# Start of a one-core transformer kernel: what each queue loads first, who issues it, and a second channel order for the router

## The chip, the core and the metric

One Trainium2 core runs the whole program in one launch. Its engines are TensorE (PE in the profile, with its weight loads shown apart as PEld), VectorE (DVE), ScalarE (ACT), GpSimd (POOL) and SyncE (SP), which here only issues transfers; 16 DMA engines move the data. Each engine runs its own instruction stream in order and waits on semaphores. The metric is the device time of one execution in microseconds, and the figure compared is the median of several executions.

## The reference

x is 256 tokens of 1024 channels in float32. What the start of the program has to do:

```python
x = x + pool_mixer(rms_norm(x, pool_norm), pool_w, pool_b, pool_scale)
x = x + hier_moe(rms_norm(x, ffn_norm[0]), router_group_w[0], ...)   # layer 0
k, k_rope, v = shared_kv(x, ...); x = x + mla_attention(...)
x = x + hier_moe(rms_norm(x, ffn_norm[1]), router_group_w[1], ...)   # layer 1
# then a second block: a mixer (S5 and mLSTM), cross attention to mem_2, a gated FFN
```

`pool_mixer` takes, for each quarter of the channels, a trailing mean (2, 4, 8 or 16 tokens) minus the token, multiplies by a 256x256 matrix, adds `pool_b` and scales by `pool_scale`. `hier_moe` chooses one of 4 groups and 2 of its 8 experts for each token from `h @ rg_w` and `h @ re_w`; each of the 32 experts computes `(silu(h @ w_gate) * (h @ w_up)) @ w_down`, 6 MiB of weights an expert. All 32 experts are computed in both layers.

## The kernel before

**Data.** Tokens lie on 128 partitions in two tiles (t = 0, 1): `X` is the residual, `XN` the normalised copy, `hT` and `pl` hold transposed activations with channels on partitions in 8 chunks k. `arena` is one large tile in which each stage has views of its own: `band` (the matrices of the trailing means, from `in_inverse_counts`), `pool_w`, `pool_b`, `pool_scale`, `memt` (the memory, from `in_mem`), `vec_rows` (small vectors, loaded as rows of 128 numbers and turned by PE into columns of `VT`), `rw` and `rb` (router weights and bias).

**Weights.** Everything large goes through `ring`, six places of 2 MiB each (a slab). SP issues the slabs in the order of their use, and before each it waits until PE has finished the slab that held the place (`slabs_done`). Slab `XK0` (a part of `x_wkv`) is first, then five expert slabs fill the ring. At each MoE some extra slabs find room outside of the ring: one in the arena (`load_ahead`, after x is ready), one over `X` once `X` is parked in DRAM (`park_x`, then `load_over_x`), one over `XN` after sorting (`load_over_sorting`, L638). From the fourth turn on the loads run in a loop.

**The first stage.** SP issues `X`, 7 small vectors, `pool_w`, then 13 more vector loads, three S5 vectors, `memt`, four router loads. Then it waits for all small vectors (`vec2_loaded`) and the pool data (`pool_loaded`), and only then issues `XK0` and the slabs. ACT issues `const`, `band`, `pool_b`, `pool_scale`, `ffn_gain` from its own queue.

The work is: ACT sums squares of X (`norm("pool")`, L1539), DVE scales it into `XN` (L1922), PE multiplies by the bands (L831, L832), DVE and ACT evict (L1931, L1550), PE multiplies by `pool_w` (L841). POOL first waits for all three pool loads, multiplies `pool_b` by `pool_scale` (L2582), waits for the S5 vectors and copies one (L2584), and adds the bias to X (L2589, two instructions). DVE waits for both and for the norm of the memory, and adds the mixer's output in four pairs (L1961, L1962). The last pair makes x ready (`x_ready`).

**Router.** PE turns X (L751, `turn(X)`, 16 transposes), turns the memory in layer 0, and multiplies by `rw` (L868). `hT[p, k]` holds channel 128k + p, so `rw` is loaded as `"(k p) g -> p k g"`: for every partition 8 pieces of 16 or 128 bytes. DVE chooses, PE counts (L885 to L889), DVE builds the selection matrices, and PE sorts the tokens (L899) and starts on the experts (L956 gate and up, L972 transposes, L1000 down, L985 combination). L899 reads `XN_rows`, where chunk c holds channels 8p + c: its weight operand has a stride of 8 numbers. L972 reads `hid_rows` with a stride of 2. In the gaps PE computes the memory's keys (L796). `keep_busy` (L818) issues matmuls whose results nobody reads.

## Time and profile before

| | us |
|---|---|
| median of 3 runs | 1698.14 (1697.07 to 1698.57) |
| the profiled execution | 1701.85 |
| its span, from first to last instruction | 1700.0 |
| PE busy | 1612.9 (95%) |
| DVE, ACT, POOL busy | 456.6, 234.5, 97.3 |
| the chain that ended last | PE 63%, DMA 30%, DVE 4%, ACT 1% |
| moved | 512.48 MB, 301 GB/s over the span |

The profile cuts the span into 40 slices of 42.5 us: through the two MoE layers the DMA engines are busy all the time at 420 to 428 GB/s; in the attention part between them and behind the second they are not. The chain of work that ended last is followed back from the last instruction: at each step to what released it. Busy time of an engine off that chain costs nothing. The profiled execution is 3.71 us longer than the median of the runs.

### The profile page before, as it was taken

The numbers are of one execution on the slowest core, as the hardware profiler recorded it, in microseconds if no ns is written. First come the engines' busy times: TensorE is split into PE (matmuls) and PEld (weight loads), VectorE is DVE, ScalarE is ACT, GpSimd is POOL, SyncE is SP. The second block draws the span as 40 slices with busy tenths as digits, with TensorE's granted clock in tenths as the row PEclk, the third lists the DMA queues.
The fourth block names the chain that finished last, engine by engine and source line by source line (L and its number), as shares of the span: only waits on it lengthen the run. The fifth ranks groups of instructions, "written<-read, shape, count | busy, mean of one in ns | idle before, by whom it ended". The sixth has DMA issues, their size and how long they took to land.

```text
span 1700.0 us, 22104 instructions
## 1 busy us (share of the span) xinstructions
PE 1612.9 (95%) x9079; PEld 1008.2 (59%) x9079; DVE 456.6 (27%) x983; ACT 234.5 (14%) x519; POOL 97.3 (6%) x165
## 2 busy tenths in 40 slices
PE   8999998888989999999998988999999998999998
PEld 7755544444446766755544444448578777688843
DVE  4311111111113323212111111115976302344411
ACT  4110100000002121111000000013122113100000
POOL 2300000000000000029200000000000000000000
PEclk9999999999999999999999999998999999999999
DMA  9999999999998643899999999998324451444400
GB/s 330 419 412 423 426 428 426 425 425 426 427 421 299 197 173 125 347 406 419 426 426 427 427 428 426 426 386 308 124 100 149 179 167 50 161 149 148 149 25 25
DMA packets 107944, 512.48 MB, mean 301 GB/s; under 512 B 17034, under 2 KB 46315, under 8 KB 74091
## 3 DMA queue, kind: packets, MB, share of 16 engines
q1 hardware_dynamic: 105595, 506.24, 74.4%
q10 hardware_dynamic: 2288, 5.40, 0.9%
q8 instruction: 41, 0.67, 0.2%
q14 instruction: 20, 0.16, 0.0%
HBM read 506.38 MB, written 5.24 MB: 301 GB/s over the span
## 4 chain that ended last, share of the span: by engine, by line
PE 63%; DMA 30%; DVE 4%; ACT 1%; SPq 1%; issue 1%; DVEq 0%; ACTq 0%
DMA ring<-in_w_up 29%; PE PS L956 15%; PE PS L1480 9%; PE PS L1000 5%; PE PS L1224 4%; PE PS L1492 4%; PE PS L985 3%; PE PS L1235 2%; PE PS L899 2%; PE PS L1430 2%; PE PS L811 2%; PE PS L1203 2%; PE PS L1407 2%; PE PS L796 1%; DMA ring<-in_x_wkv 1%; PE PS L1416 1%
## 5 line engine op out<-in xcount | busy, mean ns | idle before, releaser
L956 PE MATMUL PS<-ring,arena 128*64 128x256 f32 x3968 | 449.2, 381 | 54.8 <-DMA ring<-in_w_up 42.7
L956 PEld LDWEIGHTS PS<-ring,arena 128*64 128x64 f32 x3968 | 287.7, 137 | 236.7 <-DMA ring<-in_w_up 60.0
L1000 PE MATMUL PS<-ring,arena 128*64 128x512 f32 x992 | 226.5, 598 | 1.2 <-ACT arena L1659 1.2
L2116 DVE TENSOR_TENSOR arena<-PS,arena 128x256 f32<-128x256 f32 x64 | 27.2, 424 | 719.7 <-ACT arena L1651 719.7
L1000 PEld LDWEIGHTS PS<-ring,arena 128*64 128x64 f32 x992 | 66.2, 136 | 152.9 <-issue 152.1
L1480 PE MATMUL PS<-hT,ring 128*128 128x256 f32 x640 | 138.3, 379 | 0.0
L1480 PEld LDWEIGHTS PS<-hT,ring 128*128 128x128 f32 x640 | 121.6, 190 | 16.5
L985 PE MATMUL PS<-arena,hT 64*128 64x512 f32 x512 | 127.2, 615 | 1.2 <-ACT arena L1668 1.2
L1659 ACT ACTIVATE arena<-PS 128x256 f32<-128x256 f32 x64 | 24.6, 384 | 507.7 <-PE PS L972 507.7
L1224 PE MATMUL PS<-hT,ring 128*128 128x256 f32 x384 | 86.7, 387 | 0.0
L1224 PEld LDWEIGHTS PS<-hT,ring 128*128 128x128 f32 x384 | 74.2, 195 | 11.7 <-issue 1.5
L1668 ACT ACTIVATE arena<-PS 128x512 f32<-128x512 f32 x64 | 38.2, 597 | 306.2 <-PE PS L1000 306.2
L1492 PE MATMUL PS<-ring,arena 128*128 128x512 f32 x176 | 75.7, 592 | 0.0
L985 PEld LDWEIGHTS PS<-arena,hT 64*128 64x128 f32 x512 | 44.1, 186 | 39.9 <-issue 30.2
L1492 PEld LDWEIGHTS PS<-ring,arena 128*128 128x128 f32 x176 | 33.4, 190 | 41.7 <-issue 41.4
L2128 DVE SCALAR_TENSOR_TENSOR hT<-hT,arena 128x512 f32<-128x512 f32 x64 | 50.5, 789 | 0.4 <-PE PS L985 0.2
L2307 DVE SCALAR_TENSOR_TENSOR arena<-PS,VT,arena 128x255 f32<-128x255 f32 (+2 forms) x104 | 43.5, 476 | 1.1
L2302 DVE TENSOR_SCALAR arena<-PS,VT 128x256 f32<-128x256 f32 x48 | 23.0, 537 | 77.5 <-PE PS L1480 77.4
L2110 DVE COPY arena<-arena 128x512 f32 (+1 forms) x64 | 28.7, 449 | 29.2 <-issue 22.2
L972 PEld LDWEIGHTS PS<-const,arena 128*128 128x128 f32 x128 | 20.4, 206 | 24.8 <-issue 24.7
L899 PE MATMUL PS<-arena,XN 128*128 128x256 f32 x128 | 32.3, 409 | 1.0 <-DVE arena L2041 1.0
L899 PEld LDWEIGHTS PS<-arena,XN 128*128 128x128 f32 x128 | 31.2, 335 | 3.2 <-issue 3.0
(424 smaller groups left out, 1445.1 us busy)
## 6 DMA issues: line engine op xcount, KB each, us to landing
ring<-in_w_gate SPq DMA_DIRECT2D x62, 2048.0 KB, 25.5
ring<-in_w_up SPq DMA_DIRECT2D x62, 2048.0 KB, 25.6
ring<-in_w_down SPq DMA_DIRECT2D x62, 2048.0 KB, 24.6
ring<-in_f_w_up SPq DMA_DIRECT2D x22, 1024.0 KB, 7.4
ring<-in_w_in SPq DMA_DIRECT2D x9, 2048.0 KB, 19.0
ring<-in_f_w_down SPq DMA_DIRECT2D x5, 2048.0 KB, 7.8
arena<-in_w_gate SPq DMA_DIRECT2D x2, 2048.0 KB, 22.7
ring<-in_x_wkv SPq DMA_DIRECT2D x2, 2048.0 KB, 8.4
```

Of the source, the lines that this page charges most:

```text
L811: mm = pe.matmul(PS[:, 1, :], hT[:, k, t * P:(t + 1) * P], w[:, k, :], start=(k == 0), stop=(k == KD - 1))
L899: mm = pe.matmul(PS[:, 4 * half + c // 2, c % 2 * T:(c % 2 + 1) * T], XN_rows[:, t, c, :], sel[:, t, half * T:(half + 1) * T], start=(t == ...
L956: mm = pe.matmul(PS[half * WINDOW:(half + 1) * WINDOW, bank, m * half_f:(m + 1) * half_f], xw[bank][:, k, :], mat(k, F_EXP)[:, half * half ...
L985: mm = pe.matmul(PS[:, 4 + 2 * t + half, :], buf[rows, t * P:(t + 1) * P], y2[rows, :], start=first, stop=last, skip_group_check=True)
L1000: mm = pe.matmul(PS[half * WINDOW:(half + 1) * WINDOW, 3, :], hidT[:, w, k * WINDOW:(k + 1) * WINDOW], mat(k, D)[:, half * 512:(half + 1) ...
L1203: mm = pe.matmul(PS[:, 2 + 2 * half + t, :], oT[:, h, t * P:(t + 1) * P], w[:, h, :], start=(h == 0), stop=(h == HEADS - 1))
L1224: mm = pe.matmul(PS[:, bank + b, f % 2 * T:(f % 2 + 1) * T], w[:, k, f * P:(f + 1) * P], x[:, k, :], start=(k == 0), stop=(k == kx - 1))
L1480: mm = pe.matmul(PS[:, 2 * (j % 2) + h, f * T:(f + 1) * T], w[:, k, h, f * P:(f + 1) * P], x[:, k, :], start=(k == 0), stop=(k == KD - 1))
L1492: mm = pe.matmul(PS[:, 4 + 2 * t + half, :], gF[:, c, t * P:(t + 1) * P], w[:, c - 4 * j, half * 512:(half + 1) * 512], start=(c == 0), st ...
L1668: act.activation(y2, PS[:, 3, :], ACT.Copy).then_inc(g["y_sbuf"], 1)
L2128: dve.scalar_tensor_tensor(gates2, slots[:, 0, :], slot_of[:, w, bass.ds(linear(e, 1, 0), 1)], slots[:, 1, :], ALU.is_equal, ALU.mult).the ...
L2307: ins = dve.scalar_tensor_tensor(v, ps(f)[:, 0:T - back], taps[f][back], v, ALU.mult, ALU.add)
```

## The change

It does seven things.

- `X` is loaded in two halves, by SP and ACT, each the first transfer of its queue; both halves count on `x_loaded` (waits on it rise by one transfer).
- SP issues, behind its half, 6 small vectors and `pool_w`, and at once `XK0` and five expert slabs. Its wait for `vec2_loaded` and `pool_loaded` is gone.
- The other 13 vector loads and the three S5 vectors are issued by POOL, ahead of all its work, all on `vec2_loaded`.
- `memt` is issued by ACT behind `pool_scale`; the four router loads of layer 0 by ACT behind `norm("pool")`. Layer 1's stay with SP.
- The router rows are loaded as `"(p k) g -> p k g"`, contiguous in each partition. So `hT` of both routers must hold channel 8p + k: `turn(X, rows=X_rows)` reads X with a stride of 8 numbers, and the gain comes from `ffn_gain` instead of `VT`. `ffn_norm` leaves the small vectors.
- `eps` no longer comes with `const` but from a DVE memset into a tile of its own; ACT no longer waits for `const` before the first norm, and DVE does `norm("pool")` before it copies the first vectors.
- PE's first `keep_busy` (8 matmuls on `const`) becomes 20 matmuls on a tile that DVE sets to one.

The core of the diff (the rest moves semaphore counts by what is listed above):

```diff
-VECTORS = (("pool_norm", 8), ("ffn_norm", 16), ("kv_in_norm", 8), ("attn_norm", 8), ("kv_norm", 2),
+VECTORS = (("pool_norm", 8), ("kv_in_norm", 8), ("attn_norm", 8), ("kv_norm", 2),
...
-FIRST_VECTORS = 7
+FIRST_VECTORS = 6
+SECOND_LOADS = len(VEC_PARTS) - FIRST_VECTORS + 3
...
+        eps_at = sbuf("eps_at", [P, 1])
...
+        warm = hTf[:, 0:P]
+        X_rows = X[:, :, :].rearrange("p t (q k) -> p t k q", k=KD)
...
+        def vectors(eng, parts, loaded):
+            for name, first, at, m in parts:
+                src = a[name]
+                dims = " ".join(f"a{i}" for i in range(len(src.shape)))
+                src = src.rearrange(f"{dims} -> ({dims})").rearrange("(r p) -> r p", p=P)
+                eng.dma_start(vec_rows[at % P:at % P + m, at // P, :], src[first:first + m, :]).then_inc(s[loaded], 16)
+        def router_loads(eng, layer):
+            eng.dma_start(rw[:, :, 0:GROUPS], a["router_group_w"][layer].rearrange("(p k) g -> p k g", p=P)).then_inc(s["row_loaded"], 16)
+            eng.dma_start(rw[:, :, GROUPS:], a["router_expert_w"][layer].rearrange("(p k) g -> p k g", p=P)).then_inc(s["row_loaded"], 16)
+            eng.dma_start(rb[:, 0:GROUPS], a["router_group_b"][layer].partition_broadcast(P)).then_inc(s["row_loaded"], 16)
+            eng.dma_start(rb[:, GROUPS:], a["router_expert_b"][layer].partition_broadcast(P)).then_inc(s["row_loaded"], 16)
-            sp.dma_start(X[:, :, :], a["x"].rearrange("b (t p) d -> p (b t) d", p=P)).then_inc(s["x_loaded"], 16)
-            def vectors(parts, loaded):
-                for name, first, at, m in parts:
-                    src = a[name]
-                    dims = " ".join(f"a{i}" for i in range(len(src.shape)))
-                    src = src.rearrange(f"{dims} -> ({dims})").rearrange("(r p) -> r p", p=P)
-                    sp.dma_start(vec_rows[at % P:at % P + m, at // P, :], src[first:first + m, :]).then_inc(s[loaded], 16)
-            vectors(VEC_PARTS[:FIRST_VECTORS], "vec_loaded")
+            sp.dma_start(X[:, 0, :], a["x"].rearrange("b (t p) d -> p (b t) d", p=P)[:, 0, :]).then_inc(s["x_loaded"], 16)
+            vectors(sp, VEC_PARTS[:FIRST_VECTORS], "vec_loaded")
-            vectors(VEC_PARTS[FIRST_VECTORS:], "vec2_loaded")
-            for at, name in ((0, "s5_lam_re_2"), (S5J, "s5_lam_im_2")):
-                sp.dma_start(s5_rows[at:at + S5J, :], a[name][0].rearrange("(j g) p -> j (g p)", g=2)).then_inc(s["s5_loaded"], 16)
-            sp.dma_start(ldt2[32:32 + S5J, :], a["s5_log_dt_2"][0].rearrange("(j g) -> j g", g=2)).then_inc(s["s5_loaded"], 16)
-            def router_loads(layer):
-                sp.dma_start(rw[:, :, 0:GROUPS], a["router_group_w"][layer].rearrange("(k p) g -> p k g", p=P)).then_inc(s["row_loaded"], 16)
-                sp.dma_start(rw[:, :, GROUPS:], a["router_expert_w"][layer].rearrange("(k p) g -> p k g", p=P)).then_inc(s["row_loaded"], 16)
-                sp.dma_start(rb[:, 0:GROUPS], a["router_group_b"][layer].partition_broadcast(P)).then_inc(s["row_loaded"], 16)
-                sp.dma_start(rb[:, GROUPS:], a["router_expert_b"][layer].partition_broadcast(P)).then_inc(s["row_loaded"], 16)
-            sp.dma_start(memt, a["mem_2"].rearrange("b (t p) d -> p (b t) d", p=P)).then_inc(s["mem_loaded"], 16)
-            router_loads(0)
-            sp.wait_ge(s["vec2_loaded"], 16 * (len(VEC_PARTS) - FIRST_VECTORS))
-            sp.wait_ge(s["pool_loaded"], 16 * 3)
-                router_loads(1)
+                router_loads(sp, 1)
...
-            def turn(v, bank=4):
+            def turn(v, bank=4, rows=None):
-                            mm = pe.transpose(PS[:, bank + j, at:at + P], v[:, t, c * P:(c + 1) * P], ident)
+                            part = v[:, t, c * P:(c + 1) * P] if rows is None else rows[:, t, c, :]
+                            mm = pe.transpose(PS[:, bank + j, at:at + P], part, ident)
...
+            pe.wait_ge(s["dve_step"], 2)
+            for _ in range(20):
+                pe.matmul(PS[:, 7, 0:P], warm, warm, start=True, stop=True)
-            keep_busy(7, 8)
...
-                turn(X)
+                turn(X, rows=X_rows)
...
+            act.dma_start(X[:, 1, :], a["x"].rearrange("b (t p) d -> p (b t) d", p=P)[:, 1, :]).then_inc(s["x_loaded"], 16)
+            act.dma_start(memt, a["mem_2"].rearrange("b (t p) d -> p (b t) d", p=P)).then_inc(s["mem_loaded"], 16)
...
-            act.wait_ge(s["x_loaded"], 16)
+            act.wait_ge(s["dve_step"], 2)
+            act.wait_ge(s["x_loaded"], 32)
+            norm("pool")
+            router_loads(act, 0)
-            norm("pool")
...
-                hT_upper(name, ["ffn_norm"], KD * layer)
+                act.wait_ge(s["gain_loaded"], 16)
+                hT_upper(name, ["ffn_norm"], col=router_gain(layer))
...
-            dve.wait_ge(s["x_loaded"], 16)
+            step(dve.memset(eps, EPS))
+            step(dve.memset(warm, 1.0))
+            dve.wait_ge(s["x_loaded"], 32)
+            norm("pool")
-            norm("pool")
...
-                hT_lower(name, ["ffn_norm"], KD * layer)
+                dve.wait_ge(s["gain_loaded"], 16)
+                hT_lower(name, ["ffn_norm"], col=router_gain(layer))
...
+            vectors(pool, VEC_PARTS[FIRST_VECTORS:], "vec2_loaded")
+            for at, name in ((0, "s5_lam_re_2"), (S5J, "s5_lam_im_2")):
+                pool.dma_start(s5_rows[at:at + S5J, :], a[name][0].rearrange("(j g) p -> j (g p)", g=2)).then_inc(s["vec2_loaded"], 16)
+            pool.dma_start(ldt2[32:32 + S5J, :], a["s5_log_dt_2"][0].rearrange("(j g) -> j g", g=2)).then_inc(s["vec2_loaded"], 16)
-            pool.wait_ge(s["s5_loaded"], 16 * 3)
+            pool.wait_ge(s["vec2_loaded"], 16 * SECOND_LOADS)
```

The order on ACT's stream, from its start, before:

```order
L1525 DMA const<-in_const 128x1193
L1526 DMA arena<-in_inverse_counts 128x1536
L1527 DMA arena<-in_pool_b 128x1024
L1528 DMA arena<-in_pool_scale 128x1024
L1530 DMA ffn_gain<-in_ffn_norm 128x2x8
L1535 ACT_TABLE_LOAD [waits const_loaded]
L1535 ACTIVATE stat<-const 1x1 [waits x_loaded]
```

and after:

```order
L1519 DMA X<-in_x 128x1024
L1520 DMA const<-in_const 128x1192
L1521 DMA arena<-in_inverse_counts 128x1536
L1522 DMA arena<-in_pool_b 128x1024
L1523 DMA arena<-in_pool_scale 128x1024
L1524 DMA arena<-in_mem 128x2x1024
L1526 DMA ffn_gain<-in_ffn_norm 128x2x8
L1531 ACT_TABLE_LOAD [waits x_loaded]
L1531 ACTIVATE stat<-eps_at 1x1 [waits dve_step]
L1535 ACTIVATE XN,stat<-X 128x1024
L1537 ACTIVATE stat<-stat,eps_at 128x1 [waits norm_ssq]
L1535 ACTIVATE XN,stat<-X 128x1024
```

X's half stands ahead of `const`, the memory has come in behind `pool_scale`, and the table load now waits for `x_loaded` instead of `const_loaded`.

The order on SP's stream around `pool_w` and the first slabs, before (its tail ahead of the first slabs):

```order
L551 DMA arena<-in_s_lam_im 16x128
L552 DMA arena<-in_s_log_dt 16x2
L560 DMA arena<-in_mem 128x2x1024
L555 DMA arena<-in_router_group_w 128x8x4
L556 DMA arena<-in_router_expert_w 128x8x32
L557 DMA arena<-in_router_group_b 128x4
L558 DMA arena<-in_router_expert_b 128x32
L579 DMA ring<-in_x_wkv 128x8x384 [waits pool_loaded,vec2_loaded]
L597 DMA ring<-in_w_gate 128x4096
L597 DMA ring<-in_w_up 128x4096
```

and after, from `pool_w` on:

```order
L541 DMA arena<-in_mem_norm_g 8x128
L556 DMA arena<-in_pool_w 128x8x256
L571 DMA ring<-in_x_wkv 128x8x384
L589 DMA ring<-in_w_gate 128x4096
L589 DMA ring<-in_w_up 128x4096
L589 DMA ring<-in_w_gate 128x4096
L589 DMA ring<-in_w_up 128x4096
L589 DMA ring<-in_w_down 128x2x2048
L606 DMA x_park<-X 128x2048 [waits x_ready]
L589 DMA arena<-in_w_gate 128x4096 [waits x_ready]
```

Between `pool_w` and `ring<-in_x_wkv` no transfer and no wait is left.

The order on POOL's stream at its first arithmetic, before:

```order
L2571 UNCONDITIONAL_BRANCH [waits barrier_Pool_Activation_PE_DVE_SP_gather]
L2582 ISA
L2582 TENSOR_TENSOR arena<-arena 128x1024 [waits pool_loaded]
L2584 COPY arena<-arena 16x128 [waits s5_loaded,pool_step]
L2589 TENSOR_TENSOR X<-X,arena 128x1024 [waits norm_xn,s5_small]
```

and after (ten vector loads stand ahead of this piece):

```order
L541 DMA arena<-in_f_conv_w 127x128
L541 DMA arena<-in_f_conv_w 5x128
L541 DMA arena<-in_f_conv_b 44x128
L2588 DMA arena<-in_s_lam_re 16x128
L2588 DMA arena<-in_s_lam_im 16x128
L2589 DMA arena<-in_s_log_dt 16x2
L2591 ISA
L2591 TENSOR_TENSOR arena<-arena 128x1024 [waits pool_loaded]
L2593 COPY arena<-arena 16x128 [waits vec2_loaded,pool_step]
L2598 TENSOR_TENSOR X<-X,arena 128x1024 [waits norm_xn,s5_small]
```

The multiplication now stands behind 16 transfers that POOL issues itself, and its copy waits for all of them instead of three.

## Rows read from the trace of the kernel before

**Rows 1.** Chain that ended last, in order of time: start, us, what; first MoE.

```profile
33.08 3.50 PE PS L868 x32
...
46.63 8.01 PE PS L899 x32
...
203.01 6.93 PE PS L956 x64
...
209.96 22.67 DMA ring<-in_w_up
```

**Rows 2.** Windows: busy us of five engines with counts, granted clock, DMA share, GB/s.

```profile
core 0: us, PE busy (x) PEld busy (x) DVE busy (x) ACT busy (x) POOL busy (x), PEclk, DMA share, GB/s
4.00:8.00 4.00, 1.51 (x7) 1.51 (x8) 0.00 (x0) 1.28 (x1) 0.00 (x0) 1.00 1.02 417
...
20.00:24.00 4.00, 4.00 (x20) 3.54 (x19) 0.33 (x3) 3.17 (x9) 3.83 (x2) 1.00 0.47 72
...
100.00:104.00 4.00, 4.00 (x40) 2.61 (x38) 0.00 (x0) 0.60 (x1) 0.00 (x0) 1.00 0.90 305
...
728.00:732.00 4.00, 4.00 (x36) 2.44 (x34) 0.00 (x0) 0.60 (x1) 0.00 (x0) 1.00 0.74 238
```

**Rows 3.** SyncE issues in order of time: start, us, queue, line, transfer.

```profile
88.30 0.43 SPq L638 DMA_DIRECT2D arena<-in_w_down  x1
100.30 0.33 SPq L597 DMA_DIRECT2D ring<-in_w_gate  x1
```

**Rows 4.** Timeline, first stage: start, us, engine, line, what, [idle before <-releaser].

```profile
1.23 0.49 ACTq L1526 DMA_DIRECT2D arena<-in_inverse_counts  x1
...
2.23 0.80 ACTq L1528 DMA_DIRECT2D arena<-in_pool_scale  x1
...
6.49 3.49 PEld L818 LDWEIGHTS PS<-const 128*128 128x128 f32 x16 [6.49 <-DMA const<-in_const]
...
6.52 1.28 ACT L1535 ACT_TABLE_LOAD   x1 [6.52 <-DMA const<-in_const]
...
8.88 0.20 ACT L1535 ACTIVATE stat<-const 1x1 f32<-1x1 f32 x1 [1.08 <-DMA X<-in_x]
...
15.96 2.35 POOL L2582 TENSOR_TENSOR arena<-arena 128x1024 f32<-128x1024 f32 x1 [15.52 <-DMA arena<-in_pool_w]
...
18.81 0.28 POOL L2584 COPY arena<-arena 16x128 f32<-16x128 f32 x1 [0.50 <-DMA arena<-in_s_log_dt]
...
19.17 4.66 POOL L2589 TENSOR_TENSOR X<-X,arena 128x1024 f32<-128x1024 f32 x2
...
28.62 0.69 DVE L1962 TENSOR_TENSOR X<-X,arena 128x512 f32<-128x512 f32 x1
```

**Rows 5.** DMA issues by transfer: KB each, us from issue to landing.

```profile
arena<-in_inverse_counts ACTq DMA_DIRECT2D x1, 768.0 KB, 8.3
...
arena<-in_pool_scale ACTq DMA_DIRECT2D x1, 512.0 KB, 11.0
```

**Rows 6.** The page's part on DMA queues: kind, packets, MB, share.

```profile
q10 hardware_dynamic: 2288, 5.40, 0.9%
```

**Rows 7.** Weight loads of three lines: ns min/median/max, first and last start.

```profile
L751 PEld LDWEIGHTS PS<-const,X x48: 138/140/144, 29.4 to 662.9; 128*128 128x128 f32 x48
...
L899 PEld LDWEIGHTS PS<-arena,XN x128: 312/336/338, 46.6 to 710.8; 128*128 128x128 f32 x128
...
L972 PEld LDWEIGHTS PS<-const,arena x128: 194/198/223, 82.5 to 1136.0; 128*128 128x128 f32 x128
```

**Rows 8.** Chain that ended last, second MoE, router: start, us, what.

```profile
661.50 1.75 PE PS L751 x16
663.24 1.73 PE PS L796 x8
664.97 3.51 PE PS L868 x32
```

**Rows 9.** Windows of one us, same columns as rows 2, first router stage.

```profile
38.00:39.00 1.00, 1.00 (x4) 0.82 (x3) 0.90 (x6) 0.21 (x1) 0.00 (x0) 0.50 0.96 410
```

More of the change, by code:

```diff
@@ L121, in constants @@
     put("causal_mask", np.where(col <= row, 0.0, -BIG))
-    put("eps", np.full((P, 1), EPS))
     window_row = np.arange(P)[:, None] % WINDOW + WINDOW * np.arange(WINDOWS)[None, :]
@@ L368, in bc @@
             return v.to_broadcast([P, *shape])
-        ident, ones, eps = cc("ident"), cc("ones"), cc("eps")
+        ident, ones, eps = cc("ident"), cc("ones"), eps_at[:, 0:1]
         ssq, rms, rinv = stat[:, 0:2], stat[:, 2:4], stat[:, 4:6]
@@ L618, in load_over_x @@
                     name = ("ffn0", "ffn1")[layer]
-                    sp.wait_ge(s["x_loaded"], 16 * (2 + 2 * layer))
+                    sp.wait_ge(s["x_loaded"], 16 * (3 + 2 * layer))
                     sp.wait_ge(s["norm_xn"], TT * (SCALED.index(name) + 1))
@@ L1240, in mix @@
             def mix():
[L1241 removed]
+                pe.wait_ge(s["s5_loaded"], 16 * 9)
                 for ri in range(2):
@@ L1541, in norm, with router_gain @@
                     act.activation(rms[:, t:t + 1], ssq[:, t:t + 1], ACT.Sqrt, bias=eps, scale=1.0 / D).then_inc(s["norm_rms"], 1)
+            def router_gain(layer):
+                return lambda name, c: ffn_gain[:, layer, c:c + 1]
             def hT_upper(name, gains, at=0, dsts=(hT,), bank=4, col=vec):
@@ L1922, in norm, with router_gain @@
                         dve.tensor_scalar(XN[:, t, :], src[:, t, :], rinv[:, t:t + 1], None, ALU.mult).then_inc(s["norm_xn"], 1)
+            def router_gain(layer):
+                return lambda name, c: ffn_gain[:, layer, c:c + 1]
             def hT_lower(name, gains, at=0, dsts=(hT,), bank=4, col=vec):
@@ L2159, in experts @@
                         step_dve(dve.tensor_tensor(gains, PS[:, 0, 0:KD], VT[:, at:at + KD], ALU.mult))
-                    dve.wait_ge(s["x_loaded"], 16 * (3 + 2 * layer))
+                    dve.wait_ge(s["x_loaded"], 16 * (4 + 2 * layer))
                     dve.wait_ge(s["proj_mm"], 2 * TT + layer + 1)
```

10 lines of the change are left out of this document (3 added, 7 removed).

## Prediction, made before the changed kernel ran

> **What bounds the kernel now.** I read the chain of waits first. In the first MoE it runs over PE alone from the router (33.08) over the sort (46.63) to 203.01; from 209.96 on it waits for slabs, one of 22.67 us at first [rows 1]. So PE works on a stock of slabs early and uses it up later; behind 210 the DMA engines set the time. It looks as if 17 us of earlier slab loads must be worth 17 us. But the ring has six places, and the windows tell when it was full: from 100 to 104 us the DMA share is 0.90 and the rate 305 GB/s, where the stretch from 4 to 8 us has 1.02 and 417 [rows 2]. SP had issued at 88.30 and next at 100.30, when PE freed a place [rows 3]: DMA had nothing to do then for about a us. All later slabs queue behind that issue, so the end of the first MoE moves with the moment at which PE frees that place (100.30), and that moves with the moment at which x is ready. A slab that is there earlier only makes DMA idle longer. The second MoE has the same hole at 728 to 732 (0.74, 238 GB/s) [rows 2]. So two things count: when x is ready (29.31, the end of the last addition at 28.62 + 0.69 [rows 4]), and PE's way from there to the experts, in both layers.
>
> What makes x ready: `pool_w` lands at 15.96 and starts POOL (2.35 us, to 18.31); POOL waits 0.50 us for an S5 vector, adds the bias to X (19.17 + 4.66 = 23.83), and DVE's additions follow until 29.31 [rows 4].
>
> **How the queues share the engines.** ACT's queue moved 2288 packets [rows 6]. Its 15 transfers have 2048 contiguous pieces, and 15 x 16 completions are 240: a packet is one piece. A transfer of one piece for each of 128 partitions gives 8 to each of the 16 engines. Now the landings, per engine: ACT's 8th piece (`const`) at 6.49; X, 16 pieces on SP's queue, at 8.86 [rows 4]; ACT's 16th piece (`band`) at 1.23 + 8.3 = 9.5; the 32nd (`pool_scale`) at 2.23 + 11.0 = 13.2 [rows 4, 5]. X and ACT's 16th piece land within 0.7 us, though band's pieces are 6 KB and X's 4 KB. The queues take turns piece by piece, not byte by byte. That matters, since `pool_w` comes in 8 pieces of 1 KB a partition, 64 an engine.
>
> **Part by part.**
>
> *X in halves.* Both halves go first: 1.05 MB before anything else. X lands some 2.5 us sooner (2.36 us lay between `const` and X [rows 4]). The table load, which hid ahead of X, now waits for X and costs its 1.28 us [rows 4]. DVE no longer waits for the first vectors. The normalised X is ready 1.5 to 2 us earlier, and PE's band matmuls with it. PE then waits for `pool_w`; this gain ends there and is worth 0.
>
> *pool_w.* Behind its half of X, ACT's queue holds 8 + 8 + 8 + 8 + 16 + 16 = 64 pieces an engine (`const`, `band`, `pool_b`, `pool_scale`, memory, `ffn_gain`); SP's holds about 3 + 64. One for one they end together. Before, the memory's 1.05 MB came behind `pool_w`; now they go ahead: 1.05 MB at 417 GB/s [rows 2] is 2.5 us. POOL's own queue adds 316 short pieces, 20 an engine; at the 0.057 us of a `pool_w` piece alone ((15.96 - 13.2) / 48) this would be 1.1 us, at their bytes 0.4; I take 0.8. `pool_w` lands at 15.96 + 2.5 + 0.8 = 19.3. Below, it can't start POOL before `pool_scale`, 13.2 plus the 1.2 us of ACT's half of X: 14.4. Above: SP's queue loses more turns, 21.
>
> *POOL's 16 issues.* No row shows one. SP's take 0.33 and 0.43 us [rows 3], which for 16 gives 5 to 7 us; longer ones can't be excluded. They are hidden while they end before 19.3, up to 1.2 us each. So 0, and the wait of 0.50 us for the S5 vector goes: -0.5. The Trainium skill (DMA: Bandwidth & Descriptors, Specifications) gives the GpSimd path about 1 us to the first byte; if each issue held POOL so long they would end at 17, and the sum would be the same. No run so far shows it.
>
> *x ready:* +3.3 - 0.5 = **+2.8 us**, at 32.1. Bounds: -2.0 (14.4) and +4.5 (21).
>
> *Turning X with a stride of 8.* The operand read with a stride is PE's weight load. Contiguous, a transpose's load shows 140 ns (L751) and the pace is 1.75 / 16 = 109 ns [rows 7, 8]. With a stride of 2 (L972) it shows 198, with a stride of 8 (L899, not a transpose) 336 [rows 7], and L899's pace is 8.01 / 32 = 250 ns [rows 1], where its 256 columns alone need 216 (1.73 us for 8 in L796 [rows 8]). So the load sets 250. I take it, since stride and operand are those of the new line: 16 x (250 - 109) = **+2.2 us**. Lower bound by L972: 16 x 58 ns = 0.9. Nothing hides it: PE goes on in order to L868, whose result DVE waits for. It is paid in both layers: in the second the chain runs L751, L796, L868 without a gap [rows 8]. The Trainium skill (SBUF — State Buffer, Door 1: The DMA port swizzle) speaks of 16-byte lines in which at least two accesses are needed for full speed: a stride of 2 float32 would be free, a stride of 8 not. The trace disagrees on the first (198 against 140) and agrees on the second; by the rule the lower bound would not exist, and the sum would stand.
>
> *Router rows.* 128 short pieces an engine become 16. They land before the large slabs if ACT issues them by 12 us: ACT's 64 + 32 pieces then end ahead of SP's 3 + 64 + 64. L868 began at 33.08 before [rows 1]. Worth 0, since the ring's hole takes the freed DMA time. Layer 1's stay off the chain in the attention part.
>
> *eps, warm-up, gains, removed SP waits:* 0; they lie before `pool_w`, or touch slabs that arrive early.
>
> **Sum:** 2.8 + 2.2 (layer 0) + 2.2 (layer 1) = +7.2 us. The profiled execution would be 1701.85 + 7.2 = 1709.1; it stood 3.7 above the median, so the median becomes 1698.1 + 7.2 = **1705.3**.
>
> **Rivals.**
>
> 1. *The head start counts* (the side that is not slower). From 20 to 24 us DMA had a share of 0.47 at 72 GB/s [rows 2]: 2.1 us idle, and the rest on small router pieces. Some 4 us of slab traffic could come earlier. If the stock never fills the ring, the first MoE ends 4 us sooner whatever PE does at first: 1698.1 - 4 + 2.2 = 1696.3, or 1694.1 with a free stride. It decides where DMA had no hole before 100.30; the hole is there. 0.12, of which 0.07 below 1694.7.
> 2. *The stride is free in a transpose*: only +2.8, 1700.9. For: the 336 ns are of a plain load, and no row has a transpose with a stride of 8. Against: L972 is a transpose and pays. 0.10.
> 3. *pool_w is not late*, since ACT's queue runs behind or yields: x ready at -2.0 to 0, the stride paid twice: 1700.5 to 1702.5, say 1701.5. Against: the landings fit turns by piece within 0.7 us. 0.13.
> 4. *The clock.* At 38 to 39 us it stood at 0.50 (1.2 GHz) [rows 9], behind a stretch from 29.3 to 36.6 in which PE had only transposes and L868's 36 columns [rows 1, 4]. That stretch is now 2.2 us longer, and PE's fillers ahead of it end about when they did while x comes 2.8 us later, so it begins behind an idle PE. If the half clock takes in L868 (3.50 us [rows 1]) as well: some +3, 1708.3. 0.10.
>
> My forecast has 0.55, with 1702 to 1709 of its own.
>
> **How the numbers follow.** About 0.2% (3.4 us) is what a measurement of this kernel can tell from no change. Slower by more: forecast and rival 4 (0.65) and a part of rival 3: 0.68. Faster: 0.07 from rival 1. Same: 0.25. The lower end takes in the lower bounds of both terms (-2.0 + 0.9 + 0.9: 1697.9) and rivals 2 and 3; the upper end +4.5 + 4.4 and some clock: 1710. Outside lie rival 1 and the tails, less than 0.2.
>
> **What would show it.** POOL's multiplication starts, released by `pool_w`, near 19.3 (rival 3: before 16.5). The last addition ends near 32.1. The 16 transposes of X take 4.0 us instead of 1.75 in both layers (rival 2: under 2.5). SP's first issue out of the ring's hole comes near 105 instead of 100.30, with a lower DMA share before it (rival 1: share 1.0 throughout). `const` lands near 8, the router rows near 22. What would make it wrong: a large first slab that ACT's pieces must take turns with, if `pool_w` were ahead of them all (router rows after 35 us, much slower), or POOL issues over 1.2 us each.

## The result, and the profile of the changed kernel

| | median | lowest to highest | runs | profiled execution: time, span |
|---|---|---|---|---|
| before | 1698.16 us | 1697.07 to 1698.57 | 4 | 1701.85, 1700.0 |
| after | 1729.01 us | 1728.09 to 1729.61 | 4 | 1729.21, 1727.2 |

The changed kernel is slower: the ratio is 1.0171, with a 95% interval from 1.0153 to 1.0190. The prediction was 1705.3 us in a range of 1697.9 to 1710.0. The direction was right and the size was not: 31 us instead of 7. Of the 31, the two causes that it gave make 3: `pool_w` came late, and the stride cost nothing.

The spans lie 27.2 us apart, the medians 30.8. The profiled execution of before was 3.7 us above its median, so the traces can explain only the 27.2.

The first view is again the chain of waits, now of the changed kernel (start, us, what), in its first MoE. L863 is the router's matmul (L868 before), L950 the experts'.

```profile
19.89 37.64 DMA arena<-in_router_expert_b
57.53 0.04 issue
57.57 7.04 PE PS L863 x32
...
86.85 7.06 PE PS L950 x64
...
237.87 22.57 DMA ring<-in_w_up
```

In [rows 1] the chain ran over PE from 33.08. Here it sits on one DMA for 37.64 us: the last of the four transfers of layer 0's router rows, 16 KB on ACT's queue. PE begins its router matmuls at 57.57, and they take 7.04 us where they took 3.50.

The timeline of the first stage, the same columns as [rows 4] (L546 and L547 are the last two router loads on ACT's queue, L589 the expert slabs on SP's, L591 POOL's product, L1967 DVE's last addition, L744 the transposes of X):

```profile
4.95 10.87 SPq L589 DMA_DIRECT2D ring<-in_w_gate  x1
...
5.96 1.28 ACT L1531 ACT_TABLE_LOAD   x1 [5.96 <-DMA X<-in_x]
...
11.76 8.10 ACTq L546 DMA_DIRECT2D arena<-in_router_group_b  x1
...
19.48 2.34 POOL L2591 TENSOR_TENSOR arena<-arena 128x1024 f32<-128x1024 f32 x1 [9.47 <-DMA arena<-in_pool_w]
19.89 1.07 ACTq L547 DMA_DIRECT2D arena<-in_router_expert_b  x1
...
31.66 0.69 DVE L1967 TENSOR_TENSOR X<-X,arena 128x512 f32<-128x512 f32 x1
32.41 2.06 PE L744 MATMUL PS<-const,X 128*128 128x128 f32 x16 [1.20 <-DVE X L1967]
...
57.57 7.04 PE L863 MATMUL PS<-arena,hT 128*128 128x36 f32 x32 [21.36 <-DMA arena<-in_router_expert_b]
```

`pool_w` starts POOL at 19.48 (15.96 in [rows 4]) and x is ready at 31.66 + 0.69 = 32.35. The 16 transposes of X take 2.06 us. Then PE idles for 21.36 us, until the rows are there. Two issues stall their queues: 10.87 us on SP, 8.10 us on ACT.

The DMA issues by transfer (KB, us from issue to landing) and the page's part on queues, which answer to [rows 5] and [rows 6]:

```profile
arena<-in_router_expert_w ACTq DMA_DIRECT2D x1, 128.0 KB, 40.5
...
arena<-in_router_expert_w SPq DMA_DIRECT2D x1, 128.0 KB, 8.2
```

```profile
q10 hardware_dynamic: 5072, 7.14, 1.2%
```

The same 128 KB take 40.5 us on ACT's queue in layer 0 and 8.2 us on SP's in layer 1, ahead of SP's later slabs. ACT's queue moved 5072 packets, 2784 more than in [rows 6]. That number tells what the rows were cut into: half of X (128), memory (256), two bias rows (128 + 128) and six more completions of 16 make 736; the other 2048 are the two row matrices, 1024 each, which is 8 pieces a partition and not one.

The windows, the same columns as [rows 2]:

```profile
core 0: us, PE busy (x) PEld busy (x) DVE busy (x) ACT busy (x) POOL busy (x), PEclk, DMA share, GB/s
36.00:40.00 4.00, 0.22 (x2) 0.00 (x0) 2.24 (x6) 2.67 (x5) 0.00 (x0) 1.00 1.01 422
...
44.00:48.00 4.00, 0.00 (x0) 0.00 (x0) 0.00 (x0) 0.00 (x0) 0.00 (x0) 0.50 1.02 406
56.00:60.00 4.00, 2.43 (x12) 2.43 (x12) 0.00 (x0) 0.00 (x0) 0.00 (x0) 0.50 0.03 9
60.00:64.00 4.00, 4.00 (x21) 4.00 (x20) 0.00 (x0) 0.00 (x0) 0.00 (x0) 0.50 0.02 4
...
80.00:84.00 4.00, 4.00 (x19) 3.79 (x19) 0.84 (x3) 2.25 (x5) 0.00 (x0) 1.00 0.00 0
124.00:128.00 4.00, 4.00 (x20) 1.20 (x18) 1.51 (x3) 0.00 (x0) 0.00 (x0) 1.00 0.77 324
```

While PE waits, DMA works at full share on slabs (422 and 406 GB/s). It stops when everything is in (0.03 from 56 to 60) and stands still at 80 to 84 (0.00). The ring's last slab, issued at 17.40, landed after 32.5 us, at 49.9; the last of the router rows landed at 57.5: the slabs came first and the few bytes that PE needed came last. The granted clock falls to 0.50, the lower of PE's two levels, 1.2 GHz, while PE idles, and is still there when the router's matmuls run. That is why they take 7.04 us.

SP's issues around the ring's hole answer to [rows 3]:

```profile
116.20 0.43 SPq L630 DMA_DIRECT2D arena<-in_w_down  x1
128.21 0.33 SPq L589 DMA_DIRECT2D ring<-in_w_gate  x1
```

100.30 has become 128.21, by 27.9 us. The second MoE's router (as [rows 8]) and the weight loads of the transposes (as [rows 7]):

```profile
688.93 1.76 PE PS L744 x16
690.70 1.73 PE PS L789 x8
692.42 3.50 PE PS L863 x32
```

```profile
L744 PEld LDWEIGHTS PS<-const,X x48: 139/188/207, 32.4 to 690.3; 128*128 128x128 f32 x48
```

The 16 transposes with a stride of 8 take 1.76 us in the chain, against 1.75 without it.

### The profile page after: what moved, and what is told of

It reads as the page before. It is cut to its first block, busy times and chain, and to the rows that moved or that the text cites. A ratio compares the mean times of both kernels' runs of the same rounds, so it can differ in the third digit from the quotient of the medians.

```text
span 1727.2 us, 22153 instructions
## 1 busy us (share of the span) xinstructions
PE 1621.5 (94%) x9103; PEld 1015.7 (59%) x9103; DVE 457.6 (26%) x985; ACT 234.2 (14%) x519; POOL 106.2 (6%) x181
## 3 DMA queue, kind: packets, MB, share of 16 engines
q10 hardware_dynamic: 5072, 7.14, 1.2%
## 4 chain that ended last, share of the span: by engine, by line
PE 60%; DMA 33%; DVE 4%; ACT 1%; SPq 1%; ACTq 1%; issue 1%; DVEq 0%
DMA ring<-in_w_up 29%; PE PS L950 14%; PE PS L1474 9%; PE PS L1218 4%; PE PS L1486 4%; PE PS L994 4%; PE PS L1229 2%; DMA arena<-in_router_expert_b 2%; PE PS L979 2%; PE PS L893 2%; PE PS L1424 2%; PE PS L1197 2%; PE PS L804 2%; PE PS L1401 2%; PE PS L789 1%; DMA ring<-in_x_wkv 1%
## 5 line engine op out<-in xcount | busy, mean ns | idle before, releaser
L950 PE MATMUL PS<-ring,arena 128*64 128x256 f32 x3968 | 449.2, 381 | 55.1 <-DMA ring<-in_w_up 42.9
L950 PEld LDWEIGHTS PS<-ring,arena 128*64 128x64 f32 x3968 | 287.6, 137 | 237.0 <-DMA ring<-in_w_up 60.2
L2121 DVE TENSOR_TENSOR arena<-PS,arena 128x256 f32<-128x256 f32 x64 | 27.2, 425 | 719.2 <-ACT arena L1652 719.2
L1474 PEld LDWEIGHTS PS<-hT,ring 128*128 128x128 f32 x640 | 121.6, 190 | 16.5
L1486 PEld LDWEIGHTS PS<-ring,arena 128*128 128x128 f32 x176 | 33.4, 190 | 41.7 <-issue 41.4
L789 PE MATMUL PS<-arena,ring 128*128 128x256 f32 x128 | 32.6, 410 | 1.1 <-DMA ring<-in_x_wkv 1.1
```

The costliest lines, as they stand in the source:

```text
L789: mm = pe.matmul(PS[:, bank, col + i * T:col + (i + 1) * T], w[:, k, f * P:(f + 1) * P], x[:, k, :], start=(k == 0), stop=(k == KD - 1), s ...
L950: mm = pe.matmul(PS[half * WINDOW:(half + 1) * WINDOW, bank, m * half_f:(m + 1) * half_f], xw[bank][:, k, :], mat(k, F_EXP)[:, half * half ...
L1474: mm = pe.matmul(PS[:, 2 * (j % 2) + h, f * T:(f + 1) * T], w[:, k, h, f * P:(f + 1) * P], x[:, k, :], start=(k == 0), stop=(k == KD - 1))
L1486: mm = pe.matmul(PS[:, 4 + 2 * t + half, :], gF[:, c, t * P:(t + 1) * P], w[:, c - 4 * j, half * 512:(half + 1) * 512], start=(c == 0), st ...
```

## The experiments

What they had to tell apart: is the wait made by ACT's short pieces taking turns with SP's large ones (piece for piece), and which of three things decides it: who is in which queue, how many pieces there are, or how large the other queue's pieces are? Then each smaller term of the sum was tried by itself. Line numbers in the variants differ by a few.

All in one table. "Router" is the start of the router's first matmul in layer 0, "hole" SP's issue out of the ring's hole, "sort 2" the start of the sort in the second MoE, all in us of the profiled run. The kernel before was timed again beside each group: 1698.74 us (e1, e2, e3, e8), 1698.95 (e4, e6, e7, e9) and 1699.37 (e5, e10, e11, e12).

| run | median | ratio to before, 95% | router | hole | sort 2 |
|---|---|---|---|---|---|
| before | | | 32.92 | 100.30 | 677.70 |
| after | 1729.01 | 1.0171 [1.0153, 1.0190] | 57.57 | 128.21 | 705.73 |
| e1, rows on SP's queue | 1707.36 | 1.0052 [1.0032, 1.0072] | 37.62 | 106.41 | 682.23 |
| e2, slabs wait for rows | 1705.76 | 1.0045 [1.0028, 1.0062] | 36.13 | 103.95 | 681.57 |
| e3, slabs in 4 KB pieces | 1707.37 | 1.0049 [1.0033, 1.0065] | 36.20 | 105.23 | 683.94 |
| e8, rows in whole runs | 1704.07 | 1.0038 [1.0022, 1.0053] | 35.79 | 103.08 | 678.84 |
| e4, before, SP doesn't wait | 1699.40 | 1.0001 [0.9993, 1.0010] | 33.95 | 100.53 | 677.97 |
| e5, before, stride of 8 | 1698.66 | 1.0000 [0.9989, 1.0011] | 33.82 | 100.39 | 676.96 |
| e12, before, POOL's queue | 1700.62 | 1.0011 [1.0002, 1.0021] | 34.39 | 103.28 | 680.60 |
| e6, e1 with memory behind | 1705.23 | 1.0036 [1.0024, 1.0048] | 33.58 | 102.52 | 680.28 |
| e7, e6 with waits split | 1702.75 | 1.0027 [1.0016, 1.0037] | 31.71 | 100.70 | 675.98 |
| e9, e7 with whole runs | 1702.91 | 1.0026 [1.0014, 1.0038] | 33.03 | 101.70 | 679.08 |
| e10, e7 with more fillers | 1699.76 | 1.0002 [0.9992, 1.0012] | 31.96 | 98.58 | 674.23 |
| e11, e9 with fillers, rows on ACT | 1700.79 | 1.0009 [0.9998, 1.0020] | 33.43 | 100.06 | 675.97 |

One thing first. From the hole to the sort of the second MoE it is 575.3 to 578.7 us in all fourteen rows (577.4 before, 577.5 after). Whatever moves the hole moves all that follows, to within these 3.4 us. Times of the trace are those of one execution, medians those of 4 to 35.

### e1: the router rows on SP's queue

```diff
             sp.dma_start(pool_w, ...).then_inc(s["pool_loaded"], 16)
+            router_loads(sp, 0)
...
-            router_loads(act, 0)
```

> The changed kernel with layer 0's four router loads issued by SP between pool_w and the first slab instead of by ACT. Theory (turns): the router rows are still cut into 8 short pieces a partition, because their place in SBUF is (8 rows of 36 numbers, 4 and 32 of them filled by different loads), so ACT's queue had 144 pieces an engine left which took turns one for one with SP's 16 KB pieces until SP's stock was used up. Ahead of the slabs on SP's own queue they land near 25 us, PE's router matmuls start right behind the transposes (about 36 us instead of 57.6) at full clock, and the time is 1729.0 - 21.4 - 3.4 = about 1703 (1701 to 1705). Rival (early slabs as such): whatever the router's queue, slabs issued at 4 us crowd the rest out; the time stays over 1715.

Measured 1707.36 us, above the 1701 to 1705 expected, hole at 106.41. The wait of 21 us is gone, so the rows' place in the queues makes it. The hole is 2.5 us later than e2's, and two rows of its timeline say where:

```profile
32.60 3.44 PE L745 MATMUL PS<-const,X 128*128 128x128 f32 x16 [2.88 <-DVE X L1967]
...
65.84 6.26 PE L951 MATMUL PS<-ring,arena 128*64 128x256 f32 x55 [1.73 <-issue]
```

The transposes of X came behind 2.88 us of idle PE and took 3.44 us, not 2.06 (granted clock 0.57 from 32 to 36 us). And PE stalled for 1.73 us after the ninth matmul of the first expert, on nothing that the profile names.

### e2: SP's slabs wait for the rows

```diff
+            sp.wait_ge(s["row_loaded"], 64)
```

> The changed kernel, but SP waits for layer 0's router rows before it issues the first slab; the rows stay on ACT's queue. Theory (turns): without large pieces on the other queue the router rows land at about 25 us, 1703 us in all (1701 to 1706), since slabs that start at 26 us are still there before PE needs them. Rival (ACT's issue stall of 8.1 us at the group bias, or ACT's queue being slow by itself): the rows still land after 40 us, the slabs come later still, and the time is over 1730.

Measured 1705.76 us, as expected. The rows are still 128 + 16 short pieces an engine on ACT's queue, and still behind everything there; only SP's large ones stay away until they are in. SP's first slab is issued at 23.11, so the rows had landed by then, not at 57.5. The pieces' number alone doesn't hurt. It takes the large ones beside them.

### e3: the first four expert slabs in pieces of 4 KB

```diff
+                        for c in range(4):
+                            cols = slice(c * 1024, (c + 1) * 1024)
+                            sp.dma_start(slab(n0 + j)[:, cols], (gate, up)[m][e][:, cols])...
```

> The changed kernel with the first four expert slabs issued as four transfers each, so that their pieces are 4 KB instead of 16 KB; same bytes, same queue. Theory (turns by piece): SP's stock has 64 + 128 + 16 + 8 + 8 pieces an engine instead of 128 in all, and ACT's 144 are through when about as many of SP's are: the last router load lands near 40 us instead of 57.5, the time falls by 15 to 20 us to 1709 to 1714. Rival (turns by byte, or an issue stall): no change, 1729.

Measured 1707.37 us, faster than the 1709 to 1714 expected. Nothing is moved and nothing waits; the slabs are the same bytes, in pieces of a quarter:

```profile
arena<-in_router_expert_w ACTq DMA_DIRECT2D x1, 128.0 KB, 22.4
...
36.20 4.27 PE L870 MATMUL PS<-arena,hT 128*128 128x36 f32 x32
```

The same 128 KB land after 22.4 us, not 40.5. The last of the four row transfers lands at 36.2 (19.67 + 16.5), where 40 was expected, and PE, whose transposes end at 36.20 too, doesn't wait any more. This is the sharpest of the tests: if the queues shared by bytes, cutting SP's pieces smaller would change nothing for ACT. They take turns by piece. SP's issues also came later here (its ring was issued by 33.4 us instead of 17.8), but that didn't clear the way: from 20 to 36 us the DMA share stays at 1.04 or more and the rate at 350 to 398 GB/s, so SP's pieces were there all the time.

### e8: the rows in whole runs, into a free place

```diff
+        rstage = arena[:, 19000:19000 + KD * (GROUPS + EXPERTS)]
...
+                eng.dma_start(stage_e, a["router_expert_w"][layer].rearrange("(p k) g -> p (k g)", p=P))...
...
+            step(pool.tensor_copy(rw[:, :, GROUPS:], stage_e.rearrange("p (k g) -> p k g", k=KD)))
```

> The changed kernel with layer 0's router rows loaded to a contiguous place (one piece of 128 bytes and one of 1 KB a partition) from where GpSimd copies them into their 8 rows; still on ACT's queue, still behind the first norm. Theory (turns, and the number of pieces): 32 pieces an engine instead of 144 on ACT's queue, through before SP's first 16 KB piece; the rows land at 22 to 24 us and the time is about 1702 (1701 to 1705). Rival (the number of pieces doesn't matter, only which queue): the rows land after 45 us and the time stays over 1720.

Measured 1704.07 us, as expected. Everything stays where the change has put it, on ACT's queue and beside SP's slabs, but the place that the rows are written to is contiguous too:

```profile
q10 hardware_dynamic: 3280, 7.14, 1.1%
...
arena<-in_router_expert_b ACTq DMA_DIRECT2D x1, 16.0 KB, 10.6
```

1792 packets fewer than the changed kernel's 5072 is 2 x (1024 - 128), to the packet: one piece a partition for each matrix. The last row transfer is issued at 11.46 and lands 10.6 us later, at 22.1. The prediction had said "the router rows near 22". Its arithmetic was right for 16 pieces an engine; the changed kernel has 128. ACT's issue stall of 8.10 us is gone as well (0.62 here). x is ready at 32.11, 2.8 us later than before, and the hole at 103.08, later by the same 2.8, although SP issues the first slab at 4.76 instead of 21.46.

### e4: the kernel before, with SP's two waits taken out

```diff
-            sp.wait_ge(s["vec2_loaded"], 16 * (len(VEC_PARTS) - FIRST_VECTORS))
-            sp.wait_ge(s["pool_loaded"], 16 * 3)
```

> The kernel before without SP's two waits ahead of the slabs; everything else as before, so SP issues the keys' weights and the first slabs as soon as it has issued the router rows. Theory (the ring's hole sets the end of the first MoE): a head start of the slabs is worth nothing, 1698 within 2 us, SP's issue out of the hole still at 100.3 within 0.5, DMA share between 24 and 100 us emptier at its end. Rival 1 of the prediction (the head start counts): about 4 us faster, 1694. On turns by piece: SP's slabs are all behind the router rows on the same queue, so the rows aren't late and the router still starts at 33.1.

Measured 1.0001, hole at 100.53. In its windows DMA still has a share of 0.46 from 20 to 24 us and of 0.80 from 100 to 104, the hole. But SP issues `XK0` at 21.06, where it did so at 21.03 before: its two waits had never held the slabs up. Its own issues had, the longest of them 3.96 us for `in_router_group_b` at 16.49. So e4 gives no head start and doesn't test what one is worth. The changed kernel and e8 do: they issue the first slab 16 us earlier and the ring's last 7 us earlier, and the hole moves by what PE's path moves, 27.9 and 2.8 us.

### e5: the kernel before, with the stride alone

```diff
-                turn(X)
+                turn(X, rows=X_rows)
...
-    a["router_expert_w"][layer].rearrange("(k p) g -> p k g", p=P)
+    a["router_expert_w"][layer].rearrange("(p k) g -> p k g", p=P)
```

> The kernel before with the stride alone: transposes of X read columns 8 apart, the router rows of both layers are laid in to match, and the gain comes from ffn_gain. The prediction's step said 16 loads of 250 ns in place of 109 in both layers, +4.4 us: 1703. What the changed kernel's trace shows (1.76 us for 16) says +0.0 to +0.2: 1699, the 16 transposes of X under 2.2 us in layer 0 and 1.8 in layer 1. A third outcome: the router rows read as contiguous runs of 8 rows change their landing; it stays off the path, as before.

Measured 1.0000 [0.9989, 1.0011]. Its chain in the second MoE:

```profile
660.15 1.78 PE PS L753 x16
```

The stride costs 0.03 us for 16, in place of the 2.2 predicted. The same run says what the new order of the rows does to the transfers. SP's queue in the page of the kernel before, and then in that of e5:

```profile
q1 hardware_dynamic: 105595, 506.24, 74.4%
```

```profile
q1 hardware_dynamic: 105595, 506.24, 74.3%
```

Not one packet fewer: read as `"(p k)"`, the rows are cut into as many pieces as before.

### e12: the kernel before, with the second vectors on POOL's queue

```diff
-            vectors(VEC_PARTS[FIRST_VECTORS:], "vec2_loaded")
+            for name, first, at, m in VEC_PARTS[FIRST_VECTORS:]:
+                ...
+                pool.dma_start(vec_rows[at % P:at % P + m, at // P, :], src[first:first + m, :])...
```

> The kernel before with one part of the change alone: the nine second vectors and the S5 ones (16 transfers) are issued on GpSimd's queue at its start instead of SP's behind pool_w. Theory of the prediction: the issues take about 0.5 us each and end near 10 us, ahead of pool_w at 16, so nothing on the path moves later; pool_w at 15.96 to 16.8 and the wait of 0.50 us for an S5 vector goes: 1698 to 1699, 0 to -0.5. Rival (something of GpSimd's own queue costs time that the profiled stretch doesn't show, since the variants e6, e7 and e9 take 3 to 5 us more by their medians than their first 100 us explain): 1700 to 1703, with a wider spread of times than before.

Measured 1.0011 [1.0002, 1.0021]: 0.3 to 3.6 us slower by the interval, more than the 0 to -0.5 expected, and with no wider spread (6.6 us from lowest to highest, 7.7 for the kernel before). The timeline:

```profile
9.12 0.48 POOL L2583 DMA_DIRECT2D arena<-in_s_log_dt  x1
17.42 2.35 POOL L2585 TENSOR_TENSOR arena<-arena 128x1024 f32<-128x1024 f32 x1 [7.82 <-DMA arena<-in_pool_w]
...
39.19 5.82 PE L792 MATMUL PS<-arena,ring 128*128 128x256 f32 x14
```

POOL's issues end at 9.6 and are hidden. But `pool_w` lands at 17.42, where it landed at 15.96, 16.64 (e4) and 16.13 (e5) with those transfers on SP's queue behind it. A third queue that takes turns costs `pool_w` 0.8 to 1.5 us, from one profile of each. The 14 matmuls of the memory's keys also drew the half clock (5.82 us; e4 and e5 have 3.29, the profile of before 4.98). Of these 2.5 us some 1.9 reach the hole, which is 2.9 us later than in e5; in e5 PE waits 0.66 us for DVE behind them. That draw differs from run to run.

### e6, e7, e10: three repairs, one upon the other

```diff
 e6, upon e1
-            act.dma_start(memt, ...)
+            sp.dma_start(memt, ...)            (behind pool_w, ahead of the router rows)
 e7, upon e6
-            pool.wait_ge(s["pool_loaded"], 16 * 3)      (POOL and DVE)
+            pool.wait_ge(s["pool_loaded"], 16 * 2)
+            pe.wait_ge(s["out_stored"], 16)             (PE alone waits for pool_w)
 e10, upon e7
-                    keep_busy(7, 13)
+                    keep_busy(7, 17)
```

> The changed kernel with the router rows of layer 0 on SP's queue (as in e1) and the memory there too, behind pool_w and ahead of the router rows. What it tests: the term for pool_w, 2.5 us of it from the memory's 1.05 MB ahead of pool_w. Theory: pool_w lands near 17.0 instead of 19.68, x is ready near 30.0 instead of 32.5, SP's issue out of the ring's hole comes near 104 instead of 106.41, and the time is about 2.5 us below e1's 1707.4: 1704 to 1706. Rival (the landing of pool_w is due to the issue order or POOL's own transfers, not the memory): pool_w stays at 19 and the time at 1707.

> e6, and pool_w counted on a semaphore of its own: PE alone waits for it ahead of the pooling's matmuls, while POOL's product of pool_b and pool_scale and DVE's scaling wait only for those two vectors. Theory: POOL's product (2.35 us) goes off the path behind pool_w; the path is then pool_w, PE's matmuls, DVE, and POOL's addition of the bias to X (4.66 us, which needs no pool_w) runs before it. x is ready 2 to 5 us earlier than in e6, at 25 to 28, and the time is lower by as much: 1699 to 1703. Rival (DVE's additions or the normalised X set the end then): x ready gains under 1 us.

> e7 with 17 instead of 13 pairs of filler matmuls on PE between the pooling and the transposes of X, which closes most of the 1.16 us in which PE was idle there. Theory (the spread and the higher median of e7 against its profiled run, 1702.75 against 1699.89, come from PE's clock falling to 0.50 in some executions behind that idle stretch): the median comes down by 1 to 3 us, to 1700 to 1702, and the times spread less. Rival (the clock is lost elsewhere, or the difference is of the queues): the same as e7, 1702.8 within 1.

e6: POOL starts at 17.01 instead of 19.68 (e1), as expected: the memory's 1.05 MB ahead of `pool_w` were worth 2.7 us. The hole came to 102.52, 3.9 us before e1's, the rest being e1's half clock. By the medians it is 2.1 us less than e1.

e7 and then e10, POOL, DVE and PE in the timeline:

```profile
14.27 2.35 POOL L2591 TENSOR_TENSOR arena<-arena 128x1024 f32<-128x1024 f32 x1 [4.34 <-DMA arena<-in_pool_scale]
...
22.55 0.17 DVE L1960 RECIPROCAL stat<-stat 128x1 f32<-128x1 f32 x1 [1.13 <-ACT stat L1538]
22.63 0.69 DVE L1966 TENSOR_TENSOR arena<-PS,arena 128x512 f32<-128x512 f32 x1
...
28.09 2.04 PE L746 MATMUL PS<-const,X 128*128 128x128 f32 x16 [1.16 <-DVE X L1967]
...
60.13 6.26 PE L952 MATMUL PS<-ring,arena 128*64 128x256 f32 x55 [1.94 <-issue]
```

```profile
28.33 2.05 PE L746 MATMUL PS<-const,X 128*128 128x128 f32 x16 [0.31 <-DVE X L1967]
...
57.15 7.13 PE L952 MATMUL PS<-ring,arena 128*64 128x256 f32 x64
```

In e7, POOL's product starts with `pool_scale` at 14.27, and x is ready at 28.0, which is 1.9 us before e6 (2 to 5 were expected) and 1.3 before the kernel before. It could gain no more, for DVE now stands at the reciprocal of the memory's norm (22.55), which comes ahead of its additions; ACT starts that norm when the memory lands, at 19.58. The experts start at 56.90, 2.0 us before [rows 1]'s kernel does (58.89), and the stall of 1.94 us after the ninth matmul takes that back (from the first expert's start to the second's it is 15.14 us, 12.78 in e10): hole at 100.70.

e10 has eight more filler matmuls, and its idle stretch is 0.31 us. The stall isn't there, the hole is at 98.58, and the median is down to that of before. Of e10's gain over e7, 1.0027 to 1.0002, the trace explains the 2.1 us of the hole; the rest of 4 us isn't seen in one profile. It goes with PE's mean granted clock, whose median over the executions is 0.9925 in e7 and 0.995 in e10, which agrees with what was expected and doesn't prove it.

### e9 and e11: the rows in whole runs, and their queue

> e7, and the router rows of layer 0 loaded in contiguous runs on both sides (one piece a partition each) into a free place, with POOL spreading them into the place where PE reads them, behind its addition of the bias; everything else as e7. Theory: SP's queue has 16 row pieces an engine instead of 128, so the keys' weights and the first slabs come some us earlier and the gap of 1.7 us that e1 showed in the first experts (at 64 us) goes. Against e7: 0.5 to 3 us less, 1697 to 1701, which is within what can be told from the kernel before or just better. Rival (SP's short pieces cost nothing since the ring has a hole anyway): the same as e7, or 0.5 us more for POOL's copies if they come last before the router.

> e9 with 17 pairs of fillers, and the router rows of layer 0, in contiguous runs, on ACT's queue right behind its first normalisation (as the change has them) instead of SP's. What it tests: e1, e6, e7 and e9 alone show a stall of PE of 1.6 to 1.9 us after the ninth matmul of the first expert, and they alone have layer 0's router rows on SP's queue. Theory (that stall goes with the rows' place on SP's queue): none here, SP's issue out of the ring's hole 1.5 to 2 us ahead of e9's 101.70, and 1699 to 1701. Rival (the stall goes with when the first experts start, before 62.1 us in all its kernels but e1): it stays, and the time is e9's or e10's.

```diff
 e9, upon e7: the rows as in e8, on SP's queue
 e11, upon e9
-            router_loads(sp, 0)
+            router_loads(act, 0)               (behind ACT's first normalisation)
-                    keep_busy(7, 13)
+                    keep_busy(7, 17)
```

e9 is at e7's time, not the 0.5 to 3 us below it that were expected. x is ready 1.3 us later (29.34), since the memory lands at 20.89 instead of 19.58 and DVE stands at its norm. From the router's start to the hole e9 takes 68.7 us and e7 69.0, both with the stall: on SP's queue the 112 pieces an engine that it saves buy nothing that can be told here. The theory of an expectation, that PE's stall goes with the rows' place on SP's queue, fell with e10, which has them there and no stall. e11 has no stall either and can't tell more; its hole, 1.6 us before e9's, and its time are as expected.

## Why the prediction was wrong, step by step

The path to the first expert, from the kernel before to the changed one: x ready 29.31 to 32.35, +3.0; wait for the router rows, +21.4; the router's 32 matmuls at the lower clock, 7.04 for 3.66, +3.4. The sum is 27.8; the first expert moved by 27.9 (58.89 to 86.78 in the timelines), the hole by 27.9, the sort of the second MoE by 28.0 and the span by 27.2.

- **"128 short pieces an engine become 16" is the step that failed**, and with it "They land before the large slabs" and "Worth 0". The diff makes the rows contiguous in memory, and I took that for the whole transfer. But `rw` holds 36 columns for each k, 4 and 32 of them from two matrices, so on the side of SBUF the run ends after 16 or 128 bytes. A piece is a run that is contiguous on both sides. 5072 packets show it. In e5 the change of order alone leaves SP's queue at its 105595 packets, and e8, which changes only the place in SBUF (and adds POOL's two copies), brings the rows in at 22.1 and takes 25 us off. So the change cut no piece away: it moved the 128 an engine that there had always been to a queue beside large ones. The term that was put at 0 measured 21.4 us of waiting and, by the clock, 3.4 more. The Trainium skill (DMA: Bandwidth & Descriptors, Why a DMA increments its semaphore by 16 and not by 1) has a descriptor for one contiguous run of the last dimension, which the packets of this case bear out on both sides.
- **"The queues take turns piece by piece, not byte by byte" was right**, and is what makes the failed step so dear. Behind `pool_w`, SP had 64 + 8 + 8 + 8 + 8 + 16 + 8 + 8 = 128 pieces an engine (the keys' weights, five slabs, X's copy, one more slab), ACT 144. One for one, ACT's last come when SP has none left: 14.5 x 1.05 MB at 423 GB/s is 36 us behind 19.5, so 55.5, and they came at 57.5. The prediction named this very outcome under what would make it wrong ("router rows after 35 us, much slower"), but made it hang on `pool_w` being ahead of ACT's pieces, gave it no chance and left it outside the range. The keys' weights, 64 pieces behind `pool_w`, would have covered 32 of ACT's pieces; they can't cover 144.
- ***pool_w* was right**: 19.3 predicted, 19.48 measured; x ready 32.1 and 32.35. e6 gives 2.7 us for the memory ahead of it (2.5 taken), e12 0.8 to 1.5 for POOL's pieces (0.8 taken).
- **POOL's issues were right** in that they are hidden: 0.49 to 0.79 us each, 8.7 in all where SP's rows had given 5 to 7, and over at 10.0. The wait of 0.50 us is gone.
- **The stride was wrong**, +2.2 twice for 0 (rival 2, which had 0.10). The shown durations of the loads rose from 140 to 188 ns, but the pace stayed at 1.76 / 16 = 110 ns. I had read a pace out of L899's loads, which are of another kind of instruction, a plain matmul, though L751's own rows showed that loads of 140 ns fit into a pace of 109. Its place in SBUF cost nothing either. The rule of the Trainium skill that I had cited beside it (SBUF — State Buffer, Door 1: The DMA port swizzle) fits no better as I used it: a stride of 8 isn't seen to lose anything in a transpose.
- **The hole was right**, and is the most useful line of the prediction: all slabs were in early, DMA stood still, and the end moved by what PE's path moved. The rival "the head start counts" fell with it, and with e8.
- **Rival 4, the clock, was right in kind**: half clock in L863 was taken at +3 and measured +3.4, but because of the 21 us of idling and not because of the few us that I had in mind. In e1 it hit after 2.88 us of idling, in e6 after 2.90 it did not (the transposes took 2.04 us).

With 16 pieces an engine and a free stride, the sum would have been 1698.1 + 2.8 = 1700.9; e8 is this kernel, plus POOL's two copies. Its hole is those 2.8 us later, and it took 1704.07, 5.3 more than the kernel before beside it; the other 2.5 belong to point (1).

What stays open. (1) The medians of the changed kernel and all that come from it lie 1600.7 to 1602.7 us above the hole of their profile, those of before, e4, e5 and e12 1597.3 to 1598.9. That sets many executions beside the hole of one; with the profiled execution's own time the two groups overlap (1598.7 to 1602.1, and 1597.5 to 1601.6). PE's mean granted clock, which every execution has on record, goes with these 2 to 3 us: over the 35 executions of the kernel before beside e5, 0.001 less comes with 1.0 us more (correlation -0.81), and its median is 0.995 there, 0.9945 in e12, 0.992 in e8 and 0.9925 in e7 and e9. What lowers it isn't shown: neither the stride nor POOL's queue does, and the order of ACT's loads, the halves of X and the warm-up weren't tried alone. (2) The stall of 1.6 to 1.9 us after the ninth matmul of the first expert is in e1, e6, e7 and e9, and in none of the others. e10 differs from e7 by eight fillers on PE, so neither the queues nor DMA's load alone make it; what it waits for, the profile doesn't show. (3) Apart from (1), what remains of e8's distance from before is x ready (+2.8), mostly the memory ahead of `pool_w`, which e6 takes away; but none of the repaired kernels is faster than before beyond its interval, e10 being the best of them.

## What to carry to other kernels

Count a transfer's pieces from both of its access patterns, and check the count against the packets of the queue: 128 KB in 1024 pieces took 40.5 us beside 16 KB pieces and 9.6 in whole runs. What an engine will wait for soon must not share the DMA engines, on another queue, with a stock of large pieces; put it ahead in the same queue, or give it few pieces. And before counting a head start as a gain, find the place where the buffers were full: behind it nothing counts but the time at which the reader frees one.
